# One decoder step with mLSTM states: each 1 MB decode state moved by one load and one store, or by halves

## The reference, cut to what matters

```python
num = w_c[..., None] * jnp.einsum('bhtk,bhkv->bhtv', qc, C) + jnp.einsum('bhts,bhsv->bhtv', S, vc)
...
C_new = wL_c[..., None, None] * C + jnp.einsum('bhs,bhsk,bhsv->bhkv', wL, kc, vc)
```

## Time and profile before

| | |
|---|---|
| median of 3 runs | 2647.47 us (2646.32 to 2650.36) |
| span of the profiled execution | 2648.1 us |
| TensorE busy | 2473.5 us, 93% |
| VectorE busy | 782.2 us, 30% |
| ScalarE busy | 442.5 us, 17% |
| GpSimd busy | 120.0 us, 5% |
| loads of decode states | 64 of 512 KB, median 4.7 us from issue to landing |
| stores of decode states | 64 of 512 KB, median 4.0 us |

### The profile page before, as it was taken

The page is one execution under the profiler, slowest core; times in us unless marked ns, Lnnn a source line. Parts: engine busy times, 40 slices in busy tenths (PEclk is TensorE's granted clock), DMA queues, the critical chain, the costliest instruction groups (busy, mean ns, idle before and its releaser), DMA issues.

```text
span 2648.1 us, 26856 instructions
## 1 busy us (share of the span) xinstructions
PE 2473.5 (93%) x10008; PEld 1669.8 (63%) x10009; DVE 782.2 (30%) x1701; ACT 442.5 (17%) x674; POOL 120.0 (5%) x193
## 2 busy tenths in 40 slices
PE   8999999999699999989979999999999988999996
PEld 1487878347477788666753654736537755877765
DVE  0134344211511111244563443433432033111112
ACT  0223233210310000121121220312201030000001
POOL 0000000000100000000002011020010010000000
PEclk9999999979779999989989999999999995999998
DMA  9412121651014444221116224062242110344420
GB/s 358 174 58 73 64 73 65 216 190 64 0 48 159 159 162 162 72 83 37 51 43 221 81 98 180 24 229 73 82 165 84 64 40 0 135 159 158 159 88 37
DMA packets 77782, 290.67 MB, mean 110 GB/s; under 512 B 8912, under 2 KB 8912, under 8 KB 76928
## 3 DMA queue, kind: packets, MB, share of 16 engines
q1 hardware_dynamic: 54432, 200.57, 21.9%
q0 software_dynamic: 23264, 88.88, 9.3%
HBM read 241.94 MB, written 47.48 MB: 109 GB/s over the span
## 4 chain that ended last, share of the span: by engine, by line
PE 83%; DVE 7%; DMA 4%; ACT 3%; issue 2%; DVEq 0%; ACTq 0%; POOL 0%; SPq 0%; POOLq 0%
PE ps L409 21%; PE ps L659 15%; PE ps L668 8%; PE ps L437 6%; PE ps L627 4%; PE ps L489 3%; PE ps L865 3%; PE ps L685 3%; PE ps L421 3%; DMA arena<-in_c 2%; PE ps L874 2%; PE ps L858 2%; DMA out_mc_s<-arena 2%; PE ps L837 2%; PE ps L454 2%
## 5 line engine op out<-in xcount | busy, mean ns | idle before, releaser
L409 PE MATMUL ps<-hT,ring 128*128 128x288 f32 x1792 | 452.5, 413 | 14.9 <-ACT hT L939 11.5
L409 PEld LDWEIGHTS ps<-hT,ring 128*128 128x128 f32 x1792 | 343.7, 193 | 112.9 <-issue 12.2
L659 PE MATMUL ps<-arena,ring 128*128 x2048 | 399.4, 356 | 0.0
L659 PEld LDWEIGHTS ps<-arena,ring 128*128 128x128 f32 x2048 | 386.8, 190 | 10.4 <-issue 8.9
L668 PE MATMUL ps<-ring,arena 128*128 128x512 f32 (+1 forms) x512 | 221.0, 592 | 0.0
L409 PE MATMUL ps<-arena,ring 128*128 128x288 f32 x768 | 191.4, 413 | 3.7 <-DVE arena L1808 3.7
L409 PEld LDWEIGHTS ps<-arena,ring 128*128 128x128 f32 x768 | 148.6, 194 | 46.1 <-DVE arena L1808 4.2
L437 PE MATMUL ps<-ring,cols 128*9 128x512 f32 x384 | 169.2, 603 | 8.7 <-DMA ring<-in_wstream 8.1
L668 PEld LDWEIGHTS ps<-ring,arena 128*128 128x128 f32 (+1 forms) x512 | 90.3, 176 | 125.3 <-issue 125.3
L858 PE MATMUL ps<-arena 128*64 128x512 f32 x256 | 123.4, 612 | 17.8 <-DMA arena<-in_c 17.0
L1506 DVE TENSOR_TENSOR arena<-ps,arena 128x224 f32<-128x224 f32 x64 | 25.1, 392 | 359.0 <-PE ps L659 359.0
(11 more groups left out here) (372 smaller groups left out, 2334.1 us busy)
## 6 DMA issues: line engine op xcount, KB each, us to landing
ring<-in_wstream SPq DMA_DIRECT2D x376, 512.0 KB, 3.3
arena<-in_c POOLq DMA_DIRECT2D x64, 512.0 KB, 4.7
out_mc_s<-arena POOLq DMA_DIRECT2D x64, 512.0 KB, 4.0
arena<-in_hg POOLq DMA_DIRECT2D x8, 512.0 KB, 3.9
out_hg_s<-arena POOLq DMA_DIRECT2D x8, 512.0 KB, 2.9
out_mc_p<-arena POOLq DMA_DIRECT2D x16, 256.0 KB, 2.4
xT<-in_xT SPq DMA_DIRECT2D x1, 2304.0 KB, 16.7
x_dram<-xT POOLq DMA_DIRECT2D x1, 2304.0 KB, 9.1
```

Source lines behind the costliest of these rows:

```text
L409: mm = pe.matmul(ps[:, 2 * p + half, 0:TH], ring[:, r, c * P:(c + 1) * P], rhs(k)[:, TH * half:TH * (half + 1)], start=(k == 0), stop=(k = ...
L659: mm = pe.matmul(ps[:, 2 * p, 0:W], ring[:, r, c * P:(c + 1) * P], mo["hs"][:, c, bass.ds(at_g, W)], start=(c == 0), stop=(c == DC - 1))
```

## The change

One DMA of 1 MB takes the place of two of 512 KB, for the loads and for the stores of all 32 decode states. The semaphores `c_in` and `c_out` go from one per half to one per buffer. GpSimd waits for all four updates of a state and then stores it whole; it waits for that store and loads the next state whole. TensorE waits once, ahead of block 0.

```diff
-        c_in, c_out = ([[sem(f"{n}{u}{half}") for half in range(2)] for u in range(2)] for n in ("c_in", "c_out"))
+        c_in, c_out = ([sem(f"{n}{u}") for u in range(2)] for n in ("c_in", "c_out"))
...
-            def half_of(state, half):
-                return state[:, HT * MD // 2 * half:HT * MD // 2 * (half + 1)]
-
             for n in range(2):
-                for half in range(2):
-                    pool.dma_start(half_of(ml["C"][:, n, :], half), half_of(io["c0"][n], half)).then_inc(c_in[n][half], 16)
+                pool.dma_start(ml["C"][:, n, :], io["c0"][n]).then_inc(c_in[n], 16)
             for h in range(MH):
                 for b in range(NB):
                     n = NB * h + b
-                    for half in range(2):
-                        pool.wait_ge(s["c_done"].sem, HT * n + HT // 2 * (half + 1))
-                        pool.dma_start(half_of(out["mc_s"][n], half), half_of(ml["C"][:, n % 2, :], half)
-                                       ).then_inc(c_out[n % 2][half], 16)
+                    pool.wait_ge(s["c_done"].sem, HT * (n + 1))
+                    pool.dma_start(out["mc_s"][n], ml["C"][:, n % 2, :]).then_inc(c_out[n % 2], 16)
                     if n + 2 < NB * MH:
-                        for half in range(2):
-                            pool.wait_ge(c_out[n % 2][half], 16 * (n // 2 + 1))
-                            pool.dma_start(half_of(ml["C"][:, n % 2, :], half), half_of(io["c0"][n + 2], half)
-                                           ).then_inc(c_in[n % 2][half], 16)
+                        pool.wait_ge(c_out[n % 2], 16 * (n // 2 + 1))
+                        pool.dma_start(ml["C"][:, n % 2, :], io["c0"][n + 2]).then_inc(c_in[n % 2], 16)
...
-                        if k % 2 == 0:
-                            pe.wait_ge(c_in[n % 2][k // 2], 16 * (n // 2 + 1))
+                        if k == 0:
+                            pe.wait_ge(c_in[n % 2], 16 * (n // 2 + 1))
```

More of the change, by code:

```diff
@@ L390, in _ @@
             for u in range(2):
-                for half in range(2):
-                    pool.wait_ge(c_out[u][half], 16 * NB * MH // 2)
+                pool.wait_ge(c_out[u], 16 * NB * MH // 2)
                 pool.wait_ge(cp_out[u], 16 * MH * HT // 2)
```

## The result

The changed kernel takes 2687.87 us (median of 4 runs, 2683.56 to 2694.53) against 2647.64 for the kernel before: 1.0157 times as long, 95% interval 1.0139 to 1.0174. That is slower by 40 us, a difference of 1.6% whose interval lies clear of 1; the forecast was 2686 with a range of 2662 to 2712.

What follows compares the result with a forecast made beforehand. TensorE bounds the kernel, waiting in four heads for buffer refills. A head takes 58.5 + 3 x (3.65 + 1.7) = 74.6 us, four 298.2, 38.2 more than 260.0: forecast 2686 us, range 2662 to 2712.

Steps and rivals of the forecast that it cites:

- What bounds the kernel: TensorE holds most of the chain; the four heads hold 26 us of waiting for buffer refills, all the change could win.
- (1): GpSimd in the heads: 64 of 128 DMA issues go away, about 0.5 us each; costed at 0.
- (2): Store of a state: starts later, after all four updates, where today's second half already starts.
- (3): Store of a state: carries 1 MB and takes 4.2 us, bounds 2.9 and 5.8.
- (4): Load of a state: carries 1 MB and takes 5.2 us, bounds 3.9 and 7.8.
- (5): TensorE at a state's first matmul: waits 3.65 us before states 2, 4 and 6 of each head, twelve in all.
- (6): TensorE's clock after each new wait: falls to the lower level, adding 1.7 us per wait.
- (7): GpSimd work behind the new waits, next stores and the prompt's state stores: not held up, cost 0.
- does not shorten the next wait: Lower clock in the heads: the slower state also updates, stores and loads later by the same amount.
- Rival A: Heads: the clock stays up after the waits, +17.8 us, 2665 us; chance 0.20.
- Rival B: Heads: loads and stores collide on their shared queue, wait 5.55 us, +70.6 us, 2718 us; chance 0.15.
- Rival C: Heads: faster, as a transfer's fixed part is paid once; -13.6 us, 2634 us; chance 0.05.

Runs made afterwards that it cites:

- the run with four filling matmuls: The changed kernel plus four matmuls whose result nothing reads, ahead of TensorE's wait before states 2, 4 and 6 of each head: 2674.15 us, ratio 1.0089.
- the quarters: The kernel before with each state in loads and stores of 256 KB: both sides 2633.76 us, loads alone 2638.39, stores alone 2661.01.
- the first experiment: The kernel before, transfers still in halves, but TensorE waits for both halves ahead of a state's first matmul: 2676.67 us, ratio 1.0104.
- the runs with one whole direction: The kernel before with only the store whole (1 MB), loads in halves: 2673.23 us; with only the load whole, stores in halves: 2675.22 us.

## Why the prediction was right, point by point

- *What bounds the kernel:* right. All but 1.7 us of the difference lies in the four stretches.
- *(1) half of the issues, cost 0:* right for the issues themselves. GpSimd's time in the heads fell from 61.16 to 29.41, and the stores and loads on the path still follow each other as before. What the term does not name is that fewer issues also remove a pause: before, GpSimd pauses ahead of its 144th issue (last section), and the changed kernel has only 114 in place of 178. The head that held the pause was 5.7 us longer than the mean of the other three, so by that estimate the change gained about 5.7 us there and lost about 49 by the rest. The sum holds this unawares, since it builds the new heads up from 58.5 and takes off the whole 260.0.
- *(2) and (3) the store:* taken as 4.2 by size from two other stores, measured 4.14 in the chain and 4.1 as the median.
- *(4) the load:* taken as 5.2 from two half loads issued together, measured 5.11 in the chain.
- *(5) the wait:* 3.65 before states 2, 4 and 6, nothing before the others; measured 3.57 on the mean, twelve times. That is 42.9 in place of 43.8 us. It was right to count the refill against the due time and not the transfers' busy time.
- *(6) the clock:* the right mechanism, a term too small. Taken as 1.7 for each wait, measured 2.2 (26.3 in place of 20.4), 2.8 in the first head and 2.0 in the other three: I chose the lower of the two levels that the five rows gave, 0.66 and 0.50 over 5 us. The profiled run shows 0.58, 0.61 and 0.78 over 7 us, by which those stretches lose 2.9, 2.7 and 1.5 us; behind the first two waits the lower level lasts longer than the 5 us that I looked at. Less the slightly shorter waits, this is the difference between the predicted 38.2 and the measured 43.2 in the heads. That the median came within 2 us of the forecast is partly luck: the profiled run, whose span grew by 44.9, was the slowest of the four, and the median grew by less.
- *The sentence that the clock "does not shorten the next wait"* is true of the even states and missed the odd ones: slower matmuls before them spare them waits, 5.1 us in all in the run with four filling matmuls. Keeping the clock up gave back 16.9 of 26.3.
- *(7) who stands behind the new waits:* right as far as the rows go; no other part of the kernel changed.
- *Rival A* (clock stays up, 2665) fell by the clock's rows, and the run with four filling matmuls shows about where it would have been: 2674. *Rival B* (collisions) came true only for the odd states' stores (4.7 to 5.1 us), and there it cost nothing: the even states' path ran with store 4.1 and load 5.1, and the odd states did not wait. In the run that kept the clock up the odd states did wait. *Rival C* (the fixed part is paid once) has a true core: 1 MB lands 1.2 us later than 512 KB, not 2.9 later. But that is not enough, and the quarters show that the opposite direction wins. The Trainium skill's rule of at least 1 MiB per DMA ("DMA: Bandwidth & Descriptors", "Rules for kernel authors") is a rule for bandwidth; here the DMA engines' busy share in the heads was 0.58 to 0.67 before and 0.48 to 0.50 after, so bandwidth was not what the loop lacked.

## What to carry to other kernels

Where a buffer is stored and loaded again between two uses, price the refill as a serial path from the last update to the first use, and set it against the time at which each piece is due; larger transfers lengthen every step of that path and bring the due time forward to the first use. Before merging transfers, look whether the DMA engines are busy or the consumer waits; in the second case split the loads (here by the consumer's own blocks) and have it wait piece by piece. And price a long idle stretch of TensorE at more than its length: a dozen waits of 2.5 to 3.6 us on the mean cost another 25 us of lower clock, while 34 us of waiting in 42 short pieces cost about 2.

## What the runs showed of the hardware that was not expected

- The loss to the clock behind a wait was nearly the same in the four runs whose twelve waits before even states have means of 2.5, 2.85, 3.0 and 3.6 us: 2.1, 2.1, 2.3 and 2.2 us each. Single waits scatter more, and the length of one does not decide alone. In the changed kernel the first matmuls behind waits of 3.4 to 3.8 us took 5.1 to 6.5 us; in the first experiment they took 5.3 and 6.5 behind waits of 1.9 and 2.0; in the run with quarter stores, half a state's matmuls behind a wait of 2.2 took 1.93, full speed.
- GpSimd pauses for about 3.5 us ahead of one DMA issue, with nothing in the profile that it waited for (`issue` as the releaser). In the kernel before it is the second store of the last head, in the run with quarter loads the second store of the third head, in the run with quarter stores a load in the third head, in the run with quarters on both sides a load in the second:

```profile
1900.11 0.54 POOL L367 DMA_DIRECT2D out_mc_s<-arena  x1 [3.52 <-issue]
...
1729.14 0.54 POOL L371 DMA_DIRECT2D out_mc_s<-arena  x1 [3.43 <-issue]
...
1745.08 0.54 POOL L377 DMA_DIRECT2D arena<-in_c  x1 [3.51 <-issue]
...
1595.39 1.60 POOL L372 DMA_DIRECT2D arena<-in_c  x3 [3.07 <-issue]
```

  Counted from the start of the program, it is GpSimd's 144th DMA issue in all four, although the bytes moved by then differ. In the last two part of the idle time passes before the store that the load needs has landed; 2.96 and 2.14 us remain behind the landing. The first experiment, whose GpSimd list is that of the kernel before, has the pause at the same place, and its longest wait (6.0 us) behind it. In each of these five kernels the head that holds the pause is the longest (69.28, 65.42, 70.64, 64.89 and 77.50). In the runs with one whole direction the 144th issue lies behind the heads, and the changed kernel never reaches it. The pause's cause was not tried, and the run with quarters on both sides has two more idle stretches of this kind, of about 4 us (4.05 and 3.96), ahead of later loads.
- The time outside the heads differs between these kernels, which share that code: 2388.1 (span 2648.1 less 260.0) before, 2389.8 after the change, 2373.8 with the whole load (span 2671.2). Differences of a few us in the total are therefore read from the heads' stretches here, each from one profiled execution, and the totals only where the interval allows it.
